# Two levels of a block inverse as 64x64 diagonal blocks, inside a recurrence

## The reference, cut to what matters

```python
# one chunk of the gated delta rule, per head and direction
lower = where(strict, (kb @ k^T) * decay, 0)      # strictly lower triangular
sol   = solve_triangular(I + lower, rhs)          # = inverse(I + lower) @ rhs
u, w  = sol[..., :dv], sol[..., dv:]
v_new = u - w @ S                                 # step from chunk to chunk
o     = (q * exp(g)) @ S + attn @ v_new
S     = S * exp(g_last) + (k * exp(g_last - g))^T @ v_new
```

## Time and profile before

| what | us |
|---|---|
| median of 3 runs | 4259.11 (4254.38 to 4259.71) |
| profiled execution, time | 4252.43 |
| profiled execution, span | 4250.7 |
| PE busy | 3831.8 (90%) |
| DVE busy | 1828.4 (43%) |
| ACT busy | 967.1 (23%) |
| POOL busy | 355.9 (8%) |

### The profile page before, as it was taken

How to read it: one execution, slowest core, us unless ns; L and a number is a source line. 1 busy time by engine, 2 the same in 40 slices (tenths; PEclk the granted TensorE clock), 3 DMA queues, 4 the chain that set the end, 5 groups by cost and what they waited for, 6 DMA issues and landing times.

```text
span 4250.7 us, 50939 instructions
## 1 busy us (share of the span) xinstructions
PE 3831.8 (90%) x21420; PEld 2366.2 (56%) x21420; DVE 1828.4 (43%) x2843; ACT 967.1 (23%) x1894; POOL 355.9 (8%) x929
## 2 busy tenths in 40 slices
PE   8989899888999999788888998888888998998999
PEld 4578556874644444667766775222254433346777
DVE  3645445554212212468777441101136467515443
ACT  3411233123211111345554311000014300100000
POOL 0023001210000000000000000000040056200000
PEclk9989999999899999799997998999988999999999
DMA  5231122311498896121100336999932012231331
GB/s 204 85 110 46 50 99 73 109 58 51 170 383 338 340 383 267 69 74 61 69 30 30 102 93 250 421 421 421 383 77 66 21 47 55 72 104 50 109 95 54
DMA packets 278564, 631.32 MB, mean 149 GB/s; under 512 B 63552, under 2 KB 205376, under 8 KB 219456
## 3 DMA queue, kind: packets, MB, share of 16 engines
q1 hardware_dynamic: 275712, 627.40, 40.3%
q10 hardware_dynamic: 2624, 0.66, 0.1%
HBM read 611.75 MB, written 16.25 MB: 148 GB/s over the span
## 4 chain that ended last, share of the span: by engine, by line
PE 68%; DMA 11%; DVE 10%; ACT 3%; issue 3%; SPq 2%; POOL 2%; ACTq 0%; DVEq 0%
PE ps L1845 11%; PE ps L1558 11%; PE ps L1208 6%; PE ps L1896 5%; PE ps L1564 4%; DMA arena<-moe_w_down 4%; DMA arena<-moe_w_gate 2%; PE ps L1453 2%; PE ps L2069 2%; PE ps L1465 2%; PE ps L1711 2%; PE ps L1707 2%; PE ps L1716 2%; DMA arena<-moe_w_up 2%; DVE arena L3406 2%
## 5 line engine op out<-in xcount | busy, mean ns | idle before, releaser
L1558 PE MATMUL ps<-arena 128*64 128x512 f32 x3072 | 708.8, 601 | 79.3 <-DMA arena<-moe_w_up 22.6
L1558 PEld LDWEIGHTS ps<-arena 128*64 128x64 f32 x3072 | 207.6, 137 | 528.8 <-issue 387.2
L3144 DVE SCALAR_TENSOR_TENSOR arena<-arena,ps 128x512 f32<-128x512 f32 (+1 forms) x48 | 30.2, 657 | 525.7 <-PE ps L1558 525.7
L1208 PE MATMUL ps<-arena 128*128 128x512 f32 (+1 forms) x768 | 252.2, 486 | 3.5 <-DVE g_rows L2812 2.1
L1896 PE MATMUL ps<-arena 128*128 128x512 f32 x512 | 229.6, 605 | 5.0 <-DVE arena L3406 4.3
L3406 DVE TENSOR_TENSOR arena<-arena,ps 128x512 f32<-128x512 f32 x86 | 58.4, 687 | 370.8 <-ACT arena L2699 143.5
L1711 PE MATMUL ps<-h_first,w_rest 128*128 128x512 f32 (+1 forms) x576 | 214.1, 388 | 0.5 <-DVE arena L3303 0.5
L1208 PEld LDWEIGHTS ps<-arena 128*128 128x128 f32 x768 | 145.3, 190 | 104.7 <-issue 92.5
L1707 PE MATMUL ps<-h_second,w_rest 128*128 128x512 f32 (+1 forms) x576 | 199.3, 361 | 0.7 <-DVE h_second L3210 0.7
L3152 DVE TENSOR_TENSOR m_yx_rest<-ps,m_yx_lead 64x512 fp32r<-64x512 f32 x64 | 44.1, 689 | 362.1 <-ACT m_yc_lead L2417 205.6
L2417 ACT ACTIVATE m_yx_lead<-ps 64x512 fp32r<-64x512 f32 x64 | 37.9, 592 | 660.9 <-PE ps L1558 660.2
(11 more groups left out here) (499 smaller groups left out, 7087.4 us busy)
## 6 DMA issues: line engine op xcount, KB each, us to landing
arena<-moe_w_gate SPq DMA_DIRECT2D x128, 1024.0 KB, 9.0
arena<-moe_w_up SPq DMA_DIRECT2D x128, 1024.0 KB, 10.0
arena<-moe_w_down SPq DMA_DIRECT2D x128, 1024.0 KB, 11.4
arena<-ada_w SPq DMA_DIRECT2D x48, 1024.0 KB, 4.9
arena<-ffn_w_gate_up SPq DMA_DIRECT2D x22, 1024.0 KB, 5.1
arena<-gdn_w_in SPq DMA_DIRECT2D x16, 1024.0 KB, 9.7
arena<-w_in SPq DMA_DIRECT2D x30, 512.0 KB, 4.0
arena<-ssd_w_x SPq DMA_DIRECT2D x8, 1024.0 KB, 5.0
```

The lines of the kernel that those rows point to most:

```text
L1208: mm = pe.matmul(ps[:, 2 * (i % 2) + j, 0:nn], state.w[:, k, m * P:(m + 1) * P], hT[:, k, c0:c0 + nn], start=(k == 0), stop=(k == KD - 1))
L1558: mm = pe.matmul(ps[CAPX * h:CAPX * h + CAPX, bank, :], x[:, 0:CAPX], w[:, 512 * h:512 * h + 512], **flags)
```

## The change

The first two levels no longer multiply whole 128x128 matrices. At these levels U and T consist of blocks of at most 64 on the diagonal, so each product is done as two 64x64 products, one for rows 0 to 63 and one for rows 64 to 127, `diagonal` in the code. The two lie in opposite corners of the array. Their results go to two PSUM banks, b for the first half and b + 1 for the second; Y and the update of U use columns 0 to 255 of a bank, the update of T columns 256 to 511. DVE then handles each half by itself on 64 partitions, and for 16-wide blocks the update of U is cut once more, into two instructions. `r_y` and `r_tu` are raised once for each half. In the pairs 0 to 3 the level-1 products of unit 0 now stand behind `decays` of both units, where they stood between them.

```diff
@@ PE, level_y @@
-                        mm = pe.matmul(ps[:, b, heads[j]], rX[2 * (p % 3) + u][:, j, :], rT[z][:, j, :], start=True, stop=True)
-                    mm.then_inc(s.r_y, 1)
+                        for h, i in enumerate(diagonal):
+                            mm = pe.matmul(ps[i, b + h, 64 * j:64 * j + 64], rX[2 * (p % 3) + u][i, j, i], rT[z][i, j, i], start=True, stop=True)
+                            if j == HG - 1:
+                                mm.then_inc(s.r_y, 1)
@@ PE, level_update @@
-                        pe.matmul(ps[:, b + 1, heads[j]], rU[z][:, j, :], rY[u][:, j, :], start=True, stop=True)
-                        mm = pe.matmul(ps[:, b, heads[j]], rY[u][:, j, :], rU[z][:, j, :], start=True, stop=True)
-                    mm.then_inc(s.r_tu, 1)
+                        for h, i in enumerate(diagonal):
+                            pe.matmul(ps[i, b + h, 256 + 64 * j:256 + 64 * j + 64], rU[z][i, j, i], rY[u][i, j, i], start=True, stop=True)
+                        for h, i in enumerate(diagonal):
+                            mm = pe.matmul(ps[i, b + h, 64 * j:64 * j + 64], rY[u][i, j, i], rU[z][i, j, i], start=True, stop=True)
+                            if j == HG - 1:
+                                mm.then_inc(s.r_tu, 1)
@@ PE, the loop over pairs @@
                         if ahead:
                             decays(p + 2, u)
+                    for u in units:
                         level_y(p, u, 1)
@@ DVE, level_y @@
-                    dve.wait_ge(s.r_y, 2 * (3 * n + x) + u + 1)
-                    v.do(dve.tensor_tensor(part(rY[u], u), part(g3(own(p, u)), u), block(u), ALU.mult), s.r_ym)
+                    for h, i in enumerate(diagonal):
...
+                        dve.wait_ge(s.r_y, 10 * n + 4 * x + 2 * u + h + 1)
+                        v.do(dve.tensor_tensor(side_of(rY[u][i, :, i], x, u), side_of(bank_of(p, u, h, 0), x, u), block, ALU.mult),
+                             s.r_ym if h else None)
@@ DVE, level_update @@
-                    dve.wait_ge(s.r_tu, 2 * (3 * n + x) + u + 1)
-                    v.do(dve.tensor_tensor(half(rT[z], u), half(rT[z], u), bank(own(p, u) + 1, u), ALU.subtract))
-                    v.do(dve.scalar_tensor_tensor(out=half(rU[z], 1 - u), in0=bank(own(p, u), 1 - u), scalar=rmask[:, u, x:x + 1],
-                                                  in1=half(rU[z], 1 - u), op0=ALU.mult, op1=ALU.add), s.r_l)
+                    for h, i in enumerate(diagonal):
...
+                        dve.wait_ge(s.r_tu, 10 * n + 4 * x + 2 * u + h + 1)
+                        v.do(dve.tensor_tensor(side_of(t, x, u), side_of(t, x, u), side_of(bank_of(p, u, h, 256), x, u), ALU.subtract))
...
+                        for k in range(m):
+                            v.do(dve.scalar_tensor_tensor(out=old[:, :, k, :], in0=new[:, :, k, :], scalar=rmask[i, u, x:x + 1],
+                                                          in1=old[:, :, k, :], op0=ALU.mult, op1=ALU.add), s.r_l if h and k == m - 1 else None)
```

More of the change, by code:

```diff
@@ L1281, in scores @@
                     spread(tbl, 2 + u, b + 1).then_inc(s.r_bt, 1)
+                diagonal = (slice(0, 64), slice(64, 128))
                 def level_y(p, u, x):
@@ L2318, in recurrence @@
                         one, two = halves_(u)
-                        act.wait_ge(s.r_y, 2 * (3 * n + 2) + u + 1)
+                        act.wait_ge(s.r_y, 10 * n + 8 + u + 1)
                         a.do(act.activation(rY[u][two, :, one], ps[two, own(p, u), 0:64 * HG].rearrange("p (j c) -> p j c", j=HG), ACT.Copy), s.r_u)
@@ L2322, in recurrence @@
                         one, two = halves_(u)
-                        act.wait_ge(s.r_tu, 2 * (3 * n + 2) + u + 1)
+                        act.wait_ge(s.r_tu, 10 * n + 8 + u + 1)
                         a.do(act.activation(rU[2 * (p % 2) + u][one, :, two], ps[one, own(p, u) + 1, 0:64 * HG].rearrange("p (j c) -> p j c", j=HG),
@@ L2904, in scores @@
                     v.do(dve.tensor_tensor(rX[2 * (p % 3) + u], g3(side(p, u) + 1), rX[2 * (p % 3) + u], ALU.mult), s.r_xt)
[L2906 to L2913, removed]
@@ L2915, in level_y @@
-                def level_y(p, u, x):
-                    n, (half, bank, part, block) = hg * PAIRS + p, views(x)
-                    dve.wait_ge(s.r_y, 2 * (3 * n + x) + u + 1)
-                    v.do(dve.tensor_tensor(part(rY[u], u), part(g3(own(p, u)), u), block(u), ALU.mult), s.r_ym)
-                def level_update(p, u, x):
-                    n, (half, bank, part, block) = hg * PAIRS + p, views(x)
-                    z = 2 * (p % 2) + u
-                    dve.wait_ge(s.r_tu, 2 * (3 * n + x) + u + 1)
-                    v.do(dve.tensor_tensor(half(rT[z], u), half(rT[z], u), bank(own(p, u) + 1, u), ALU.subtract))
-                    v.do(dve.scalar_tensor_tensor(out=half(rU[z], 1 - u), in0=bank(own(p, u), 1 - u), scalar=rmask[:, u, x:x + 1],
-                                                  in1=half(rU[z], 1 - u), op0=ALU.mult, op1=ALU.add), s.r_l)
+                diagonal = (slice(0, 64), slice(64, 128))
@@ new lines, in side_of, with bank_of @@
+                def side_of(y, x, odd):
+                    return y.rearrange("p j (n two b) -> p j n two b", two=2, b=1 << LEVELS[x])[:, :, :, odd, :]
+                def bank_of(p, u, h, at):
+                    return ps[diagonal[h], own(p, u) + h, at:at + 64 * HG].rearrange("p (j c) -> p j c", j=HG)
+                def level_y(p, u, x):
+                    n, w = hg * PAIRS + p, 1 << LEVELS[x]
+                    for h, i in enumerate(diagonal):
+                        block = bmask[i, u, x, 32 * h:32 * h + 32].rearrange("p (n b) -> p n b", b=w).unsqueeze(1).to_broadcast([64, HG, 32 // w, w])
+                        dve.wait_ge(s.r_y, 10 * n + 4 * x + 2 * u + h + 1)
+                        v.do(dve.tensor_tensor(side_of(rY[u][i, :, i], x, u), side_of(bank_of(p, u, h, 0), x, u), block, ALU.mult),
+                             s.r_ym if h else None)
@@ new lines, in level_update @@
+                def level_update(p, u, x):
+                    n, z = hg * PAIRS + p, 2 * (p % 2) + u
+                    for h, i in enumerate(diagonal):
+                        t, uu = rT[z][i, :, i], rU[z][i, :, i]
+                        dve.wait_ge(s.r_tu, 10 * n + 4 * x + 2 * u + h + 1)
+                        v.do(dve.tensor_tensor(side_of(t, x, u), side_of(t, x, u), side_of(bank_of(p, u, h, 256), x, u), ALU.subtract))
+                        old, new, m = side_of(uu, x, 1 - u), side_of(bank_of(p, u, h, 0), x, 1 - u), 32 >> LEVELS[x]
+                        for k in range(m):
+                            v.do(dve.scalar_tensor_tensor(out=old[:, :, k, :], in0=new[:, :, k, :], scalar=rmask[i, u, x:x + 1],
+                                                          in1=old[:, :, k, :], op0=ALU.mult, op1=ALU.add), s.r_l if h and k == m - 1 else None)
```

## The result

The changed kernel takes 4270.14 us (median of 8 runs, 4261.82 to 4274.75) against 4255.39 us for the kernel before, measured again beside it (8 runs, 4245.65 to 4259.71). The ratio is 1.0036 with a 95% interval of 1.0025 to 1.0046: 15 us slower, where 0.8 us faster was forecast. The profiled execution took 4272.5 us for a span of 4270.8, 20.1 us more than the profiled span of before.

A forecast was written before the change was run, and what follows sets the result against it. The low chain's loads and DVE's pace were taken to let little of PE's saving through: 3.7 us faster without clock changes, 0.8 us with the clock falling in about half the pairs, so about 4258 us, range 4249 to 4267.

The forecast's parts named there:

- What bounds the kernel: Low chain's loads limit any gain up to pair 5: at most 1.6 us in the first run, nothing in the second.
- PE's saving: Level products of the first two levels: 64x64 ones at 0.076 us each, 3.4 us less PE work in a pair.
- DVE's cost: Masks and updates in smaller instructions: 1.8 us more DVE work per pair; the twelve small ones together 2.4 us.
- DVE reaches that point at 8.2 now: Pairs 2 and 3: DVE lets the second `decays` start 8.2 us into the pair, where it was 8.49.
- 0.45 us saved: Pairs 2 and 3, which build ahead: net saving with the moved level-1 product, without any change of clock.
- 1.05 us each of pairs 4 and 5: Pairs with nothing built ahead: 1.05 us of PE's 3.4 saved, as DVE sets the pace in the first half.
- The sum without the clock: Both runs, clock unchanged: after the low chain's limit, 3.7 us faster together.
- I take half of them at 1.7: New PE gaps in eight pairs, 2 to 5: clock loss between 0 and 1.7 us each, an average of 0.85.
- the clock falls in every pair: Rival, 17%: PE drops to the lower clock in each of pairs 2 to 5; 4264 us.
- The clock falls and stays down: Rival, 9%: PE at half rate from the gap to the pair's end; 20 to 30 us slower, about 4283.
- the two rivals on PE's saving: PE's whole saving arrives (5%), 8.4 us faster, 4251; or small products do not run side by side (3%), about 4295.
- The signs: Expected: pair 5 of the second run within 1 us of 899.3; wrong if a pair loses over 3 us to the clock.

The follow-up runs named there:

- e7_before_warm2: The kernel before with 40 products whose results nobody uses put ahead of pair 2, where PE waits for a load; ratio to before 0.9994 (0.9985 to 1.0002).
- e4_filled: The changed kernel with PE's gaps filled by products nobody reads, in `decays` and in pairs 4 and 5; ratio to the kernel before 0.9999 (0.9988 to 1.0009).
- e3_dve_split: The kernel before with only DVE's masks and updates cut as in the change, PE untouched; ratio to before 1.0024 (1.0012 to 1.0037).
- e1_order_back: The changed kernel with the level-1 product of unit 0 put back between the two `decays`; ratio to the kernel before 1.0024 (1.0012 to 1.0035).
- e2_order_alone: The kernel before with only the reordering, both `decays` and then both level-1 products, still whole; ratio to before 1.0022 (1.0011 to 1.0033).
- e9_before_best: The kernel before, whole products, plus 40 unused products ahead of pair 2 and unit 0's transposes moved earlier in pairs 4 and 5; ratio 0.9987 (0.9978 to 0.9996).

## Why the prediction was wrong, point by point

**What bounds the kernel**: right. All gains before pair 2 are lost in the wait (it is 10.59 us in the first run after), the low chain had little slack, and e7_before_warm2 ran into it at about 1 us in each run, where 1.6 and next to none were worked out. But this bounds a gain, and there was none.

**PE's saving**: the mechanism right, the size too small. 32 products of an update of both units take from 358.18 to about 360.1, 0.058 us each, where 0.076 was taken from the last level. The saving is 2 x 2 x (0.43 + 0.86) = 5.2 us a pair and not 3.4. What came earlier from it went into waits for DVE: in pair 3 there is one of 0.81 us before the first `decays`, where there was none.

**DVE's cost**: 2.4 us was worked out for the twelve instructions of the level-0 updates and 2.86 measured. The subtraction cost 0.20 as expected, a 64-wide scaled one 0.245 instead of 0.20 (the prediction's own upper value was 0.28), and the step from one half to the next adds a little. The second `decays` was forecast at 8.2 us into pair 3 and came at 9.24. Half of this is the 2.86 us; the rest is that the first `states` ended at 4.0 instead of 3.8 and the second took 2.19 us (363.70 to 365.89) instead of 2.0. That is the first failed step: "DVE reaches that point at 8.2 now". With it the "0.45 us saved" in pairs 2 and 3 becomes 1.1 us lost in pair 3 (34.2 against 33.2 in e4_filled), and the 1.05 us each of pairs 4 and 5 become 0.1 to 0.4. The sum without the clock was 3.7 us faster, and the run that shows it, e4_filled, is equal to before: 0 (5 us faster to 4 slower), with one fall left in it. The two changes of an engine's work cancel: DVE's cut alone costs 10 us (e3_dve_split).

**The clock**: the second failed step, "I take half of them at 1.7". All eight pairs fell and each cost 0.7 to 3.2 us, 15 us in all by e4_filled, where 8 x 0.85 = 6.8 were put. The two steps weigh about the same: in the other direction stood savings of 2 x (1.45 + 0.45 + 1.05 + 1.05) = 8.0 us in the eight pairs, and none came. Both halves of the step on the clock failed. The gap in pairs 1 to 3 was worked out as 2.8 us (5.4 to 8.2) and was 3.41 in pair 3 (5.83 to 9.24), for DVE was a full us later than thought and PE only 0.4; that lies beside the 3.54 us of the earlier trace rows, which had fallen. In pair 4 I counted two products of 0.61 us as work that might keep the clock, and it fell there too, for longer: the stretches above stand at 0.50 from 402 to 411 us. And the upper price of 1.7 us was that of eight products. The fall in pair 4 lasts some 10 us, and what PE does meanwhile takes nearly twice as long (a transpose 0.21 us from start to start instead of 0.11).

The Trainium skill (TensorE: Matmul & The Clock Gate, "Why this matters for your kernels") has the rule that gaps between bursts of matmuls cost the clock, and it was weighed and set at 17%. The trace agrees with it in the main: before the second `decays` of pairs 2 and 3 the clock fell behind each wait of 2.76 us or more (3.41 and 3.15 us among them) and stayed behind those of 1.66 to 1.81 us in e3_dve_split and 2.34 us in e1_order_back. But the length of the wait does not settle it, for the 1.50 us of e2_order_alone were enough once. The Trainium skill (TensorEngine Tiling (Array Packing), "PSUM Bottleneck") says that tiling speeds up TensorE but not the reading of its results, and e3_dve_split and e9_before_best bear this out: DVE's part costs 10 us where PE's saving brings as much.

**The rivals**: the first, "the clock falls in every pair", was what happened, but it gave 5.3 us slower and 15 were measured. Its clock was near (1.7 us a pair against 1.9); what failed in it were the savings that it set against the clock. "The clock falls and stays down" did not happen, and the two rivals on PE's saving were no matter.

**The signs**: one of those for "wrong" came, a pair that lost more than 3 us to the clock (3.2 in pair 4 of the second run). Pair 5 of the second run did not start within 1 us of 899.3 with a wait of 2 to 4 us for its load, but at 920.46 with none.

**Still open**: whether e2_order_alone costs the 9 us of its ratio or the 4.7 of its pairs; why its wait of 1.50 us dropped the clock once; and whether in pairs 4 and 5 the waits or the thin work between them did it.

## What to carry to other kernels

Before shortening an engine's work, ask who is the next to be waited for, and then how long the wait becomes: here PE got rid of 5 us of work a pair while DVE, which already set the pace there, got more, and PE paid for the idle time with its clock. Where a dependence keeps PE waiting in every turn of a loop, for 3 us here, fill the wait with useful work that stands later in the order; if there is none, useless products were worth 15 us here, and cost 10 where no wait was. Cutting a result over two banks to please PE at least doubles the instructions of the engine that reads it, and a DVE subtraction on half the partitions and half the width costs 0.20 us where the whole one costs 0.33.

## What the runs showed of the hardware

Two 64x64 float32 products in the upper left and lower right corners of the array cost 0.058 us each in a row, 0.117 for the two against 0.224 for one whole product, where the last level's products in the other two corners cost 0.076 each in the same kernels. No kernel here has a 64x64 product by itself; if one costs half of a whole one, 0.112 us (an estimate), the two run side by side. The Trainium skill (TensorEngine Tiling (Array Packing), "Theoretical Speedup") gives up to 2x for a dimension of 64, and by that estimate the trace agrees for the first arrangement. What makes the second slower no run here tells.

A PE that waits 10 us for a load comes back at a granted clock of 0.50 and pays 2.8 us in the 36 that follow; forty useless products in the wait take this away (36.0 to 33.3 us), if they end close to the load: with 1.92 us left between them the clock stayed in the first run of e7_before_warm2, with 2.67 us in the second it fell.
